# Expert weights on two queues: the down weights move from the sync engine's queue to ScalarE's

## What is computed

```python
def hier_moe(h, w_rg, b_rg, w_re, b_re, w_gate, w_up, w_down):
    ...
        a = jnp.einsum('sd,edf->sef', hs, w_gate)
        b = jnp.einsum('sd,edf->sef', hs, w_up)
        act = jax.nn.silu(a) * b * gates[:, :, None].astype(a.dtype)
        return jnp.einsum('sef,efd->sd', act, w_down)
```

## Time and profile before

| | us |
|---|---|
| median of three runs (lowest, highest) | 1291.29 (1287.98, 1291.51) |
| the profiled execution, its own time | 1291.53 |
| its span in the profile | 1289.9 |
| TensorE busy in the span | 1182.8 |
| VectorE busy | 672.3 |
| ScalarE busy | 356.3 |
| GpSimd busy | 212.8 |

### The profile page before, as it was taken

How to read it: one execution, slowest core, us unless ns; L and a number is a source line. 1 busy time by engine, 2 the same in 40 slices (tenths; PEclk the granted TensorE clock), 3 DMA queues, 4 the chain that set the end, 5 groups by cost and what they waited for, 6 DMA issues and landing times. The chain is left out here.

```text
span 1289.9 us, 19011 instructions
## 1 busy us (share of the span) xinstructions
PE 1182.8 (92%) x7174; PEld 662.3 (51%) x7175; DVE 672.3 (52%) x1313; ACT 356.3 (28%) x781; POOL 212.8 (16%) x250
## 2 busy tenths in 40 slices
PE   4999999999978997899999999899976999977995
PEld 1555555555543556666677776555543433332331
DVE  1255443554465884567777775544462554433443
ACT  1122222222222444265555553323320000000000
POOL 4000000000000002254443322011022212211111
PEclk9899999999998998889999999899977999988998
DMA  8721211111137871421111005362447999999993
GB/s 361 297 66 33 66 53 46 53 45 54 41 122 226 300 275 58 124 58 30 29 29 30 2 1 165 121 231 89 184 152 285 337 367 367 382 395 377 357 348 65
DMA packets 92834, 213.47 MB, mean 165 GB/s; under 512 B 20673, under 2 KB 54707, under 8 KB 77394
## 3 DMA queue, kind: packets, MB, share of 16 engines
q1 hardware_dynamic: 82258, 195.02, 41.1%
q0 software_dynamic: 7200, 17.33, 5.4%
q10 hardware_dynamic: 3296, 0.02, 0.1%
HBM read 185.03 MB, written 34.13 MB: 170 GB/s over the span
## 5 line engine op out<-in xcount | busy, mean ns | idle before, releaser
L2404 PE MATMUL g_GU<-w_gu,first_region 128*32 128x512 f32 (+2 forms) x656 | 143.0, 624 | 17.0 <-issue 17.0
L1921 PE MATMUL f_C<-first_region,oT 128*128 128x512 f32 x256 | 115.2, 603 | 0.0
L454 PE MATMUL U<-region,b_hT 128*128 128x512 f32 x256 | 112.3, 592 | 0.0
L2614 DVE TENSOR_TENSOR g_sig<-g_GU,g_sig 128x256 f32<-128x256 f32 x23 | 9.8, 425 | 165.8 <-ACT g_sig L2564 157.7
L1723 DVE TENSOR_TENSOR_SCAN region<-region,early 128x128 f32<-128x128 f32 (+7 forms) x64 | 88.6, 1404 | 6.3 <-POOL region L1530 6.3
L2404 PEld LDWEIGHTS g_GU<-w_gu,first_region 128*32 128x32 f32 (+2 forms) x656 | 43.2, 127 | 84.3 <-issue 83.4
L454 PE MATMUL b_UL<-region,b_hT 128*128 128x384 f32 (+1 forms) x256 | 76.5, 458 | 3.3 <-DMA region<-w_in 3.3
L1921 PEld LDWEIGHTS f_C<-first_region,oT 128*128 128x128 f32 x256 | 48.0, 193 | 54.3 <-issue 54.2
L454 PEld LDWEIGHTS U<-region,b_hT 128*128 128x128 f32 x256 | 47.5, 190 | 54.2 <-issue 54.0
L2383 POOL DMA_INDIRECT y<-oT,g_li x23 | 36.4, 1584 | 227.0 <-DVE oT L2632 133.8
L1592 PE MATMUL e_Z<-first_region,region 104*128 104x512 f32 (+3 forms) x192 | 70.8, 507 | 0.1
(11 more groups left out here) (489 smaller groups left out, 2160.2 us busy)
## 6 DMA issues: line engine op xcount, KB each, us to landing
w_gu<-w_gate SPq DMA_DIRECT2D x21, 1024.0 KB
w_gu<-w_up SPq DMA_DIRECT2D x21, 1024.0 KB
w_down<-w_down SPq DMA_DIRECT2D x21, 1024.0 KB
region<-w_ada SPq DMA_DIRECT2D x16, 1024.0 KB, 7.0
region<-w_in SPq DMA_DIRECT2D x3, 2048.0 KB, 17.5
oT<-w_gate SPq DMA_DIRECT2D x6, 1024.0 KB
oT<-w_up SPq DMA_DIRECT2D x6, 1024.0 KB
oT<-w_down SPq DMA_DIRECT2D x6, 1024.0 KB, 20.2
```

What stands on the lines that cost most here:

```text
L454: end = nc.tensor.matmul(dst[0:T, 0:c1 - c0], lhsT=hT[:, k, 0:T], rhs=g.w_in[:, k, c0:c1], start=k == 0, stop=k == KD - 1)
L1921: end = nc.tensor.matmul(C[n % 2][:, c * 512:(c + 1) * 512], lhsT=g.oT[:, i, k, :], rhs=wo[:, k, c * 512:(c + 1) * 512], start=k == 0, sto ...
L2404: end = nc.tensor.matmul(GU[h * n:h * n + n, :], lhsT=xT[:, b, k, h * n:h * n + n], rhs=wgu[s][:, :, k, :], start=k == 0, stop=k == KD - 1 ...
L2614: mark(nc.vector.tensor_tensor(sig[:], GU[:, 0:DE], sig[:], ALU.mult))
```

## The change

The sync engine waits for GU(instead) and issues gate and up, and nothing else. ScalarE issues the down weights. Those of the two experts whose place is free from the start (the fifth and sixth of the order) go out after the lists of blocks 2 to 8, before ScalarE's first turn. Each of the other 26 goes out in turn b = instead+1, after the copy of the hidden rows and the issue of that turn's list, behind a wait for Y(instead). Buffers, amounts and the work of all engines on data stay the same.

```diff
@@ -2443,9 +2443,6 @@
                 if instead[p] is not None:
                     sp.wait_ge(gu_mm, instead[p] + 1)
                 load_gate_up(nc, io, g, sp, expert(p), s, wgu_in[s])
-                if instead[p] is not None:
-                    sp.wait_ge(dn_mm, instead[p] + 1)
-                load_down(nc, io, g, sp, expert(p), s, wd_in[s])
 
             sp.wait_ge(xg_in[0], 16)
             for p in order[FIXED:]:
@@ -2582,6 +2579,15 @@
             act.wait_ge(xg_in[0], 16)
             for b in range(2, AHEAD):
                 list_in(b)
+
+            late = order[FIXED:]
+
+            def down_in(p):
+                load_down(nc, io, g, act, expert(p), place[p], wd_in[place[p]])
+
+            for p in late:
+                if instead[p] is None:
+                    down_in(p)
             for b in range(NB):
                 act.wait_ge(gu_mm, b + 1)
                 if b:
@@ -2593,6 +2599,10 @@
                 hidden_out(b % 2).then_inc(hT_done, 1)
                 if b + AHEAD < NB:
                     list_in(b + AHEAD)
+                for p in late:
+                    if b and instead[p] == b - 1:
+                        act.wait_ge(dn_mm, b)
+                        down_in(p)
 
             def long_body(e, row, n):
                 act.wait_ge(l_gu, n + 1)
```

## The result

| | us | ratio to the kernel before, 95% interval |
|---|---|---|
| kernel before, median of the same runs | 1291.4 | |
| kernel after, median of 6 runs (1293.95 to 1300.72) | 1296.69 | 1.005 (1.0038 to 1.0062) |
| kernel after, once more (e10) | 1295.9 | 1.0047 (1.0032 to 1.0063) |
| profiled execution, own time and span | 1300.72, 1299.0 | |

The change makes the kernel slower by some 5 to 6 us; the forecast was +9. The profiled execution happens to be the slowest of its six, 9.2 us above the one of before, so it shows more of a loss than the medians do.

What follows compares the result with a forecast made beforehand. It took TensorE and the DMA engines as full in the expert stage, with 17.0 us of waits for weights. 0 + 0 + 6.4 (order) + 2.6 (slower clock) = +9.0 on 1291.53 gave 1300 us, range 1287 to 1306.

Steps and rivals of the forecast that it cites:

- the likeliest case: Whole kernel: slower as summed, 1300 us, 1296 to 1305; chance 0.54.
- the 2 to 3 transfers too many: DMA queues before GU(19): down transfers from ScalarE's queue that pass GU(19)'s up weights, 2.5 x 2.54 = 6.4 us.
- Gate and up earlier: Sync engine: no stand at Y(instead), GU(19)'s weights issued nearly 18 us earlier; worth up to 5.3 us, taken as 0.
- one DMA engine is behind all others and has no gap: DMA engines, expert stage: the slowest has a full queue either way, so earlier issue is worth 0; an inference.
- Order, 6.4 us: DMA queues before GU(19): ScalarE's queue takes turns with the sync engine's, so down weights overtake; +6.4 us, from above 10.2.
- a down transfer lands soon: ScalarE's queue: with 128 rows like a list, which lands 6.7 us after issue, a down transfer lands soon too.
- Slower clock, 2.6 us: TensorE at GU(19): a wait grown to 7.8 us makes the product behind it slower, +2.6 us.
- Shifts of the earlier waits: TensorE: waits may shift among GU(13), GU(15) and GU(16) by a few us; up to 7.8 us end before GU(19).
- ScalarE, 0: ScalarE: 28 more issues, some 10 us, hide in idle time, two early ones in 1.49 us before the first sigmoid; cost 0.
- The rival "no change": Whole kernel: two queues deliver in nearly the old order, overtaking and early issue cancel; 1291, 3 either way; chance 0.20.
- The size of a turn: DMA engines: with packets of 9 to 17 descriptors per turn the order term would be 3 transfers, 7.6 us, not 6.4.

Runs made afterwards that it cites:

- e10: The kernel after, unchanged, run once more on one chip beside two other versions; 1295.9 us, ratio 1.0047 to the kernel before.
- e1: Against the kernel before: one queue kept, but gate and up issued as soon as GU(instead) is done; 1289.68 us, ratio 0.9995.
- e8: Against the kernel after: ScalarE issues each down load in the turn before its expert's first block, up to 3 turns later; 1288.43 us, ratio 0.9995.
- e6: Against the kernel after: down loads of 26 experts cut to a thirty-second, issues and waits kept, layer not computed; 1264.56 us, ratio 0.9802.
- e2: Against the kernel after: the sync engine again waits for Y(instead) before the next expert's gate, second queue kept; 1294.08 us, ratio 1.0024.
- e3: Against the kernel after: lists of blocks 9 to 22 issued by the sync engine behind gate and up, not by ScalarE; 1296.38 us, ratio 1.0034.
- e4: Against the kernel before: one queue, in TensorE's order of need, a block's down weights after the next block's gate and up; 1288.28 us, ratio 0.9981.
- e11: e4 repeated unchanged, on one chip with e10 and e12; ratio 0.9982 to the kernel before.
- e12: e8 repeated unchanged, on one chip with e10 and e11; ratio 0.9982 to the kernel before.

## Why the prediction was right, and where not

The kernel came out 5.3 us slower by the medians, where +9.0 was summed: inside the range, and at the low edge of the 1296 to 1305 of the likeliest case. That the profiled execution took 1300.72 us, next to the 1300 of the forecast, is luck; it was the slowest of six, and 1.5 us of it come from ahead of the stage.

*Direction and mechanism: right.* The step that decided, order, is borne out from both sides. e1 leaves the gain of early issue at nothing, e8 takes the passing away on the same two queues and the loss is gone, e6 clears ScalarE, and the 2 to 3 transfers too many are the 2.7 that ScalarE's queue moved before 1234 us. One rival is cleared only in part: e8 also brought GpSimd's additions back to 10.9 us (1045 to 1160 us). That slower additions aren't the cause rests on the chains of the kernel after, which don't pass through them.

*Gate and up earlier, taken at 0: right.* Those of GU(19) went out 24.9 us earlier (the prediction had nearly 18) and it bought nothing, on one queue (0.9995) as on two. That one DMA engine is behind all others and has no gap fits everything here, the filled gaps of e1 above all; no view shows the DMA engines one by one, so it stays an inference.

*Order, 6.4 us: somewhat high.* Inside the stage GU(19) moved by 5.2 us in the profiled execution, 5.0 in e2 and 4.8 in e10. The premise that a down transfer lands soon was wrong: 17.0 us. It didn't matter: with 10.7 us in e3 the time stayed nearly the same.

*Slower clock, 2.6 us: high.* The product behind the wait took 2.0 us more here and 8.58 - 7.07 = 1.5 more in e10, with waits of 6.85 and 4.43. The stretch from 1202 to 1250 was granted 0.93, where it had been 1.00. The length of a wait doesn't settle this cost: 3.03 us cost 1.7 in the kernel before, and 8.16 us cost 2.1 here. Sum of both terms as measured, 7.2 in the first profile; the medians, over many runs, say 5.3.

*Shifts of the earlier waits, "by a few us": too small.* The wait before GU(13), 7.34 us, is gone altogether, and those before GU(15) and GU(16) have grown by 5 each. In sum they cancel with the slow products behind them: GU(16) ends 1.3 us later than before (1198.82 against 1197.50), less than the 1.5 from ahead of the stage. So here the loss does arise at GU(19). In e2 and e10 more of it lies in the earlier waits; what agrees in all three is when GU(19) starts.

*ScalarE, 0: right for the time, wrong in one place.* In e10 the stage started with other timing, and its chain runs through the issues ahead of the first sigmoid:

```profile
983.84 0.36 ACTq L2284
...
984.75 1.28 ACT L2561
```

The two early down issues stand there on the chain with about 1 us. The prediction hid them behind 1.49 us of idle time, which this execution did not have. Whether that microsecond reaches the end isn't shown; TensorE later waits for weights in any case, which may take it up.

*The rival "no change" by the rule that more issuing engines don't help* (the Trainium skill, "DMA: Bandwidth & Descriptors", "Rules for kernel authors") was right about bandwidth: from 1130 to 1190 the share of the DMA engines is 1.02 in both kernels, with 390 and 386 GB/s. The time didn't follow bandwidth: order was worth 0.5% one way (the kernel after) and, by the ratios, 0.2% the other (e4).

*The size of a turn.* The prediction's estimate of 7.6 us went by whole packets of typically 9 to 17 descriptors per turn (the Trainium skill, same page, "Queues, rings and completion order"). No run shows the size of a turn. That lists of 1 KB delay the down transfers behind them by 6.3 us (17.0 against 10.7) rules out turns by bytes. It doesn't tell turns of one row from longer ones, since a list has 128 rows, as many as a down transfer.

*Two slips in reading.* Y(3) starts at 1033.48 in the kernel before; 1021.85 is Y(2). And the "about 64 us of TensorE work" behind GU(19)'s start are 62.5 us of the span, of which the last 16.7, behind GU(22), hold little work of TensorE. Neither enters the sum.

## What to carry to other kernels

When the DMA engines are full, as here with shares of 1.00 to 1.03, a second queue moves no more bytes, it takes turns with the first. What is on the shorter queue goes ahead of its time, and what the compute engine needs next is late: 2.7 transfers too many were 5 us here. Keep the transfers on one queue in the order in which the consumer waits for them (0.9981 and 0.9982 in e4 and e11), or delay the issues on the second queue to just before their use (0.9995 and 0.9982 in e8 and e12). An idle share of 6 to 20% of the DMA engines doesn't say that earlier issue pays: e1 filled it and gained nothing that can be told.

## What the runs showed that I had not expected

List loads of 1 KB slow the megabyte behind them in the same queue: down transfers landed in 17.0 us with the lists ahead of them and in 10.7 without (e3). And a third party was slowed: GpSimd's additions went from 10.3 to 12.5 us (1045 to 1160 us), though nothing about them had changed. It isn't the use of three queues as such, since with the same transfers on the same queues, only issued later (e8), they landed after 10.9 us. Why the time of issue makes that difference wasn't tested.
